# Hybrid RWKV/SSD/attention backbone on one core: the modulation sums beside the first RWKV layer's projections by transposed blocks, row sums and a band product

## What is computed

```python
silu_c = jax.nn.silu(c)
silu_cc = jax.nn.silu(c_ctx)
for i in range(DEPTH):
    ml = jnp.split((silu_c @ ada_w[i] + ada_b[i])[:, None, :], 6, axis=-1)
    mc = jnp.split(silu_cc @ ada_w[i] + ada_b[i], 6, axis=-1)
    hl = modulate(xl, norm1_g[i], ml[0], ml[1])
    hc = modulate(xc, norm1_g[i], mc[0], mc[1])
    ...
```

```python
dx = token_shift_centred(h) - h
xr, xw, xk, xv, xa, xg = (h + dx * mu[i] for i in range(6))
r = heads(xr @ wr); k = xk @ wk; v = heads(xv @ wv)
... xw @ w1[d] ... xa @ a1[d] ... xg @ g1
```

## Time and profile before

| what | value |
|---|---|
| median of 3 runs | 3931.67 us (3929.08 to 3935.01) |
| the profiled execution's own time | 3929.94 us |
| its span, first to last instruction | 3928.3 us |
| PE busy | 3809.7 us, 97% |
| DVE busy | 2364.5 us, 60% |
| ACT busy | 1303.0 us, 33% |
| POOL busy | 299.6 us, 8% |
| mean granted TensorE clock | 0.990 |

### The profile page before, as it was taken

How to read it: one execution, slowest core, us unless ns; L and a number is a source line. 1 busy time by engine, 2 the same in 40 slices (tenths; PEclk the granted TensorE clock), 3 DMA queues, 4 the chain that set the end, 5 groups by cost and what they waited for, 6 DMA issues and landing times.

```text
span 3928.3 us, 83381 instructions
## 1 busy us (share of the span) xinstructions
PE 3809.7 (97%) x32803; PEld 2313.1 (59%) x32803; DVE 2364.5 (60%) x4233; ACT 1303.0 (33%) x2511; POOL 299.6 (8%) x246
## 2 busy tenths in 40 slices
PE   6999999999999999999999999999999999999998
PEld 2559888644445454545444456554444458888787
DVE  7947777487743667663877235477842437776431
ACT  4036666221101455531111014321100237775311
POOL 2001101000000233220000000000000000000000
PEclk8999999999999999999999999999999999999999
DMA  5620000054432333222444320144432320000354
GB/s 198 211 60 4 4 4 15 26 160 146 154 94 74 105 99 97 78 78 91 160 154 127 101 67 28 36 136 159 140 112 79 94 68 4 4 4 15 102 152 132
DMA packets 480958, 350.64 MB, mean 89 GB/s; under 512 B 24849, under 2 KB 450137, under 8 KB 478457
## 3 DMA queue, kind: packets, MB, share of 16 engines
q1 hardware_dynamic: 454632, 235.94, 20.8%
q0 software_dynamic: 26000, 110.06, 7.8%
HBM read 344.76 MB, written 1.18 MB: 88 GB/s over the span
## 4 chain that ended last, share of the span: by engine, by line
PE 80%; DVE 11%; ACT 6%; issue 1%; SPq 1%; DMA 1%; DVEq 0%; POOL 0%; ACTq 0%; POOLq 0%
PE PS L249 38%; PE PS L950 17%; PE PS L1948 15%; PE PS L1059 2%; PE PS L584 2%; ACT WORK L2220 1%; PE PS L1107 1%; DVE WORK L1686 1%; DVE WORK L1689 1%; DVE WORK L425 1%; PE PS L1428 1%; PE PS L1119 1%; DVE WORK L1713 1%; ACT WORK L1571 1%; DVE WORK L654 1%
## 5 line engine op out<-in xcount | busy, mean ns | idle before, releaser
L249 PE MATMUL PS<-H,WR 128*128 128x512 f32 (+1 forms) x3440 | 1350.7, 552 | 2.8 <-DVE WORK L862 2.8
L249 PEld LDWEIGHTS PS<-H,WR 128*128 128x128 f32 x3440 | 648.6, 190 | 657.4 <-issue 630.6
L950 PE MATMUL PS<-BIG,WR 128*128 128x512 f32 (+1 forms) x1736 | 669.6, 543 | 4.7 <-DVE X L926 2.6
L1948 PE MATMUL PS<-WORK 64*64 64x64 f32 (+2 forms) x13088 | 571.3, 225 | 15.6 <-ACT WORK L2220 9.6
L1948 PEld LDWEIGHTS PS<-WORK 64*64 64x64 f32 (+1 forms) x13088 | 480.0, 136 | 95.8 <-ACT WORK L2220 30.7
L950 PEld LDWEIGHTS PS<-BIG,WR 128*128 128x128 f32 x1736 | 326.4, 190 | 319.5 <-issue 300.9
L425 DVE SCALAR_TENSOR_TENSOR WORK<-WORK,SC 128x512 f32<-128x512 f32 (+1 forms) x630 | 406.5, 645 | 22.4
L847 ACT ACTIVATE WORK<-PS,WORK 128x512 f32<-128x512 f32 (+1 forms) x176 | 111.8, 635 | 842.0 <-DVE WORK L877 583.4
L2220 ACT ACTIVATE WORK<-PS 128x256 f32<-128x256 f32 (+3 forms) x720 | 244.6, 340 | 233.8 <-PE PS L1948 215.8
L926 DVE SCALAR_TENSOR_TENSOR X<-PS,MOD,X 128x256 f32<-128x256 f32 x96 | 46.5, 484 | 423.6 <-PE PS L950 417.3
L860 DVE SCALAR_TENSOR_TENSOR WORK<-PS,WORK 128x510 f32<-128x510 f32 (+1 forms) x176 | 120.1, 682 | 186.3 <-ACT WORK L847 177.4
(11 more groups left out here) (281 smaller groups left out, 4624.0 us busy)
## 6 DMA issues: line engine op xcount, KB each, us to landing
WR<-in_ffn_w_in_dram SPq DMA_DIRECT2D x352, 256.0 KB, 2.9
WORK<-in_ada_w_dram POOLq DMA_DIRECT2D x33, 2048.0 KB, 8.9
WR<-in_ffn_w_out_dram SPq DMA_DIRECT2D x160, 256.0 KB, 2.7
WR<-in_ssd_w_in_dram SPq DMA_DIRECT2D x96, 256.0 KB, 2.8
WORK<-in_ada_w_dram POOLq DMA_DIRECT2D x16, 1024.0 KB, 5.9
BIG<-scratch_dram POOLq DMA_DIRECT2D x8, 2048.0 KB, 8.2
BIG<-in_ada_w_dram SPq DMA_DIRECT2D x4, 2048.0 KB, 18.6
WR<-in_rw_wk_dram SPq DMA_DIRECT2D x32, 256.0 KB, 2.8
```

Of the source, the lines that this page charges most:

```text
L249: mm = pe.matmul(outs, WR[:, slot, k, 0:m], rhs(k), start=first and k == 0, stop=last and k == nk - 1)
L950: mm = pe.matmul(PS[:, bank, lo:T], WR[:, opened[label], k, :], rhs(8 * r + k), start=r == 0 and k == 0, stop=last and k == nk - 1)
L1948: return pe.matmul(o, lhs, rhs, start=start, stop=stop)
```

## The change

The rides of layer 0 take the FFN's form: behind each ride DVE makes a transpose of the accumulator (two inputs x 512 columns, as one of 128x1024) and a row sum, and PE makes four band products in place of the eight with the ones. PE waits for the label of the row sum, `rsum`, in place of that of the ride. There are a buffer of its own for the transpose, two for the row sums in turn, and one for a band, which DVE makes ahead of the first ride. The FFN's functions only take their buffers and labels as arguments; they do what they did.

```diff
--- before.py
+++ after.py
@@ -505,22 +505,30 @@
         ROWSUM = WORK[:, 10240:10272]
         BAND = WORK[:, 10272:10272 + 96]
 
-        def band():
+
+        MIX_TURNED = WORK[:, 11264:12288]
+        MIX_ROWSUM = [WORK[:, 12288 + 32 * n:12320 + 32 * n] for n in range(2)]
+        MIX_BAND = WORK[:, 12352:12448]
+
+        def band(dst):
             eye = half_const("id64")
-            v(vec.memset(BAND, 0.0))
-            v(vec.tensor_tensor(BAND[:, 32:64], eye[:, 0:32], eye[:, 32:64], ALU.add))
-
-        def turned_sum(tag, i):
-            v(vec.transpose(TURNED, ACC[:, 0].rearrange("p s c -> p (s c)")), None, i)
-            v(vec.reduce_sum(ROWSUM, TURNED.rearrange("p (b j) -> p b j", j=32), axis=AX_X), f"{tag}.rows", i)
+            v(vec.memset(dst, 0.0))
+            v(vec.tensor_tensor(dst[:, 32:64], eye[:, 0:32], eye[:, 32:64], ALU.add))
+
+        def turned_sum(acc, turned, rowsum, label, i):
+            v(vec.transpose(turned, acc.rearrange("p s c -> p (s c)")), None, i)
+            v(vec.reduce_sum(rowsum, turned.rearrange("p (b j) -> p b j", j=32), axis=AX_X), label, i)
+
+        def four_groups(bank, rowsum, window):
+            by_block = rowsum.rearrange("p (s m j) -> p j m s", s=2, m=4)
+            for j in range(4):
+                out, low = PS[64 * (j // 2):64 * (j // 2) + 64, bank, 0:8], 32 - 32 * (j % 2)
+                mm = pe.matmul(out, window[:, low:low + 64], by_block[:, j], start=j % 2 == 0, stop=j % 2 == 1)
+            return mm
 
         def ride_pe4(tag, i):
             pe.wait_ge(vec_done, C.at(f"{tag}.rows", i))
-            by_block = ROWSUM.rearrange("p (s m j) -> p j m s", s=2, m=4)
-            for j in range(4):
-                out, low = PS[64 * (j // 2):64 * (j // 2) + 64, ABANK, 0:8], 32 - 32 * (j % 2)
-                mm = pe.matmul(out, BAND[:, low:low + 64], by_block[:, j], start=j % 2 == 0, stop=j % 2 == 1)
-            mm.then_inc(pe_done, C.mark(pe_done, f"{tag}.a"))
+            four_groups(ABANK, ROWSUM, BAND).then_inc(pe_done, C.mark(pe_done, f"{tag}.a"))
 
         def ride_pe(tag, i, n):
             pe.wait_ge(vec_done, C.at(f"{tag}.acc", i))
@@ -867,11 +875,11 @@
             v(vec.tensor_copy(CW[:, 0:66], columns(3 * l + 1, 0, 66)))
             v(vec.tensor_copy(CW[:, 66:132], columns(3 * l + 2, 0, 66)), f"f{l}.cw")
             taps3 = CW[:, 0:132].rearrange("p (t h f) -> p h f t", t=3, h=2)
-            band()
+            band(BAND)
             with C.loop(vec, f"f{l}", NF // 2) as i:
                 if l + 1 < DEPTH:
                     ride_sum(f"f{l}", i, 4)
-                    turned_sum(f"f{l}", i)
+                    turned_sum(ACC[:, 0], TURNED, ROWSUM, f"f{l}.rows", i)
                 vec.wait_ge(act_done, C.at(f"f{l}.c11", i, 1))
                 for h in range(2):
                     v(vec.tensor_copy(CWj[:, :, h, :], taps3[:, h, bass.ds(i * 2, 2), :]), f"f{l}.cwj" if h else None, i)
@@ -2151,10 +2159,10 @@
                 done(mm(PS[:, 6, lo:T], G2A[:, j * P:j * P + P], GS[:, lo:T]), f"t{j}.gate")
 
             def ride(j):
-                pe.wait_ge(vec_done, C.at(f"{t}.ride{j}"))
+                pe.wait_ge(vec_done, C.at(f"{t}.rsum{j}"))
                 if j:
                     pe.wait_ge(vec_done, C.at(f"{t}.rows{j - 1}"))
-                done(over_partitions(5, ACC[:, j % 2], 4), f"rode{j}")
+                done(four_groups(5, MIX_ROWSUM[j % 2], MIX_BAND), f"rode{j}")
 
             opened = {}
 
@@ -2417,11 +2425,14 @@
                             v(vec.tensor_scalar(acc[:, s_], w, by, None, ALU.mult), label)
                         else:
                             v(vec.scalar_tensor_tensor(acc[:, s_], w, by, acc[:, s_], ALU.mult, ALU.add), label)
+                turned_sum(acc, MIX_TURNED, MIX_ROWSUM[r % 2], f"{t}.rsum{r}", None)
 
             def ride_rows(r):
                 vec.wait_ge(pe_done, C.at(f"{t}.rode{r}"))
                 mod_rows(0, 16 + 4 * r, 4, PS[:, 5, 0:8], f"{t}.rows{r}", None)
 
+            if l == 0:
+                band(MIX_BAND)
             for r in range(4):
                 if l == 0:
                     ride(r)
```

## The result

The changed kernel takes 3942.81 us (median of 7 runs, 3940.91 to 3948.65); the kernel before, in 7 runs, 3932.44 (3929.08 to 3935.82). The ratio is 1.0033 with a 95% interval of 1.0024 to 1.0042, so it is slower by 9 to 17 us; 12.3 were forecast. The profiled execution took 3941.99 us.

A forecast was written before the change was run, and what follows sets the result against it. It took PE and DVE as two engines at one speed in the first layer's projections. Queue +10.5 and clock +1.8 made 12.3 on the median 3931.67, thus 3944 us; range 3939 to 3948.5.

The forecast's parts named there:

- PE's slot falls to 0.34 and PE does not get it: Layer 0's rides: PE's slot falls from 1.70 to 0.34 us, 10.9 saved in all, yet PE waits for DVE.
- DVE's turn is 2.53 us a ride with no spread, its band 0.40: Layer 0's rides on DVE: transpose plus row sum add 2.53 us each, 20.3 in all; the band once, 0.40.
- Two waits: PE idles for DVE's mix of input 6: 12.8 us in projection w, 5.4 to 7.5 in g.
- The clock, + 1.8 (1.2 to 3.3): PE's clock falls to half behind both waits; hidden after the first, paid after the second: +1.8 us, bounds 1.2 and 3.3.
- the dense row: PE's matmuls from 74.91 us: 50 took 23.42 instead of 21.63 us, 1.8 lost for 3.9 us at 0.56.
- the sparse one: PE behind a 6.8 us idle stretch ending at 3046.78: clock 0.50 for 7.1 us, 6.5 busy; upper bound 3.3.
- + 10.5 by the queue: First layer's projections: DVE's added work delays its mixes, so v starts at 225.9 instead of 215.4 us.
- PE would set the pace: First rival: in the first layer's projections DVE's additions are hidden, v 7.9 us earlier, 3924 us; chance 4%.
- The clock stays up: Rival: DVE's delay in the first layer comes as worked out, without PE's clock falling, 3942 us; chance 10%.
- Part is given back later: Rival: a later stage, waiting for something else than PE, returns part: +4 to +8, 3936 to 3940 us; chance 6%.

The follow-up runs named there:

- e8_act_only: Changed kernel with all eight sums in the old form and ACT making each ride's two multiply-only products; ratio 0.9988 to the kernel before.
- e3_fill: The filled kernel: changed kernel with 13 and 5 unread PE products ahead of input 6 of w and of g; ratio 1.0024 to the kernel before.
- e4_first: Changed kernel with the new form in rides 0 to 3 only, the old in 4 to 7; ratio 1.0020 to the kernel before.
- e1_pe_only: Changed kernel without DVE's transposes and row sums, PE's band products reading 32 accumulator columns directly; ratio 0.9982 to the kernel before.
- e2_dve_only: Changed kernel with DVE's transposes and row sums made but unused, PE's sums in the old form; ratio 1.0023 to the kernel before.
- e6_two: Changed kernel with the new form in rides 5 and 6 only; ratio 0.9980 to the kernel before.
- e7_act: Changed kernel with the new form in rides 4 to 7 only and ACT making each ride's two multiply-only products; ratio 0.9982 to the kernel before.
- e5_last: Changed kernel with the new form in rides 4 to 7 only; ratio 0.9997 to the kernel before.

## Why the prediction was right, step by step

- *PE's slot falls to 0.34 and PE does not get it.* Held: 0.34, and DVE's half alone with PE's old form was no slower. The saving per ride was put too high: two units and a ride take 14.28 us in the trace after (98.22 to 112.50) and 15.52 before (99.87 to 115.39), so 1.24 a ride and 9.9 in all, not 1.36 and 10.9. The slot alone doesn't show that the two units, from their start to the next ride's product, take 13.93 us in place of 13.82. The + 10.5 hardly rests on it, since DVE sets both moments.
- *DVE's turn is 2.53 us a ride with no spread, its band 0.40.* Held: 1.245 and 1.220 again, and zero to input 6 of g is 225.11 - 76.18 = 148.93 us; forecast 223.8 - 74.87 = 148.9.
- *Two waits.* Held in place, with the third of 0.54 us not foreseen; w 13.49 for 12.8, g 4.70 for 5.4 to 7.5. In the profile after, the clock had not fallen at zero (21.73 us for 50 matmuls, where before they took 23.42), so PE was earlier at w, and it was at half speed longer behind the first wait (5.9 us, not 3.9), so it was later at g. Neither moved v, since DVE set both moments.
- *The clock, + 1.8 (1.2 to 3.3).* The mechanism was right, the size was low: 5.9 us at 0.50 behind the second wait, and 2.8 us between the changed kernel and the filled one. I had taken the dense row, 3.9 us at 0.56; the sparse one, 7.1 us, was as near. Its count of idle stretches is short, too: the four it names did have the clock at 0.50 behind them, but the trace has two more of over 3 us at its start (3.42 and 6.79 us, the latter ending at 10.46) with a granted clock of 1.00 behind them. By durations that value is doubtful: six matmuls of L333 took 4.29 us at 10.46 and 2.74 us at 37.24.
- *+ 10.5 by the queue.* 10.7 with the clock kept up.
- *PE would set the pace* (the first rival, priced - 7.9): it needs DVE's additions to cost nothing; with them left out it gives - 5.0, since even DVE's old queue takes the first half's slots.
- *The clock stays up*, as a rival: v would be at + 10.5; it was at + 12.7. *Part is given back later*: from the scan on the profiled execution is shorter by 2.8 us than it was before (13.5 + 1.3 at zero against 12.0 in the span). So it is in part luck that the forecast of 12.3 lies so near the measured 10.4 (by the medians): the clock cost 1 us more than forecast, and outside the stretch something was given back that was forecast at nothing. Before, the clock was 0.83 from 680 to 700 us, and it was 1.00 in the same work after:

```profile
680.00:700.00 20.00, 18.70 (x438) 0.83 0.01 3
```

```profile
694.00:714.00 20.00, 18.59 (x510) 1.00 0.01 3
```

These rows, of before and of after, are from the recurrence of layer 0, where no edit was made. Of the other profiled kernels one has the fall at the same place (e8_act_only, 0.83 from 680 to 700), two have it some 12 us later, as their stretch is (e3_fill, e4_first), and five don't have it; each has falls elsewhere, the changed kernel too (0.83 from 3240 to 3260). Such a fall can move a single execution by some us (0.83 over 20 us of nearly dense work is an estimated 3.4 us), and that is why the sizes above are taken inside the stretch. It was not tested whether these falls follow from the change; and the timed medians of most kernels lie up to 5 us below what their stretch alone would give (+ 10.4 for + 13.5, - 3.4 for 0.0, - 8.4 for - 3.1), which stays open. The clock elsewhere may be a part: over the runs of the kernel before, a mean granted clock lower by 0.001 goes with 2.4 us more, and e8_act_only's mean is 0.0007 higher than that of the kernel before, an estimated 1.7 of its 3.4 us.

The rule of the Trainium skill (Perfetto Trace Analysis, Identifying the Most-Contended Engine), read as the prediction's rival reads it, by PE's matmul share over the whole kernel, gave the wrong sign. For PE the section itself doesn't take that share as the measure of headroom; it names MFU (the share of the peak matmul rate) and the share of weight loads, and the latter was 59% against DVE's 60%, by which PE doesn't stand out. The same page's section Optimization Strategy speaks of regimes in which another engine is the contended one, and that fits this trace: in a period here DVE was busy 14.56 of 15.30 us, though PE was busy in all of it, and the change put 2.53 us more on DVE and took 1.24 from PE.

## What to carry to other kernels

Before moving work from the engine that never waits to one that waits a little, add up, between one hand-over and the next, what the second engine has left: here 1.3 us before w's last input against 10.5 added, while over the whole kernel it was idle 40% of the time. Do as many moves as that room holds (two of eight gained 2.5 us in the stretch, eight lost 12.7), or make room on a third engine first. And price a new wait of PE with the half-speed stretch behind it, here 5.9 us, thus some 3 us more than the wait.

## What the runs showed of the hardware that was not expected

The wait's length alone did not tell whether the clock fell: PE's waits of 2.33 and 2.80 us in the filled kernel left it at 1.00, as one of 2.59 did before, but in the kernel with PE's half alone waits of 2.48 and 0.39 us, with two matmuls between, were followed by 0.50 from 139 to 142 us. Around zero PE has short waits too: seven of 0.20 to 1.03 us between 62.8 and 74.9 us in the kernel before, with 1.1 to 2.1 us of work between. There the granted clock was 1.00 from 66 us on and fell at 75, with PE working without a break from 74.91 on. It fell so in four of the ten profiled kernels (23.3 to 23.4 us from zero to ride 0's product: before, e1_pe_only, e2_dve_only, e8_act_only). In e4_first, e6_two and e7_act it fell between 71 and 73 us, some 3 us before zero, and was back by zero; in the changed kernel, e3_fill and e5_last it was low until 71 to 74 us and stayed up from there. In these six the same work took 21.6 to 21.7 us. So the 1.7 us are a matter of when the fall comes, not of whether. And filling two waits with 18 products that nobody reads gave back 2.8 us of the stretch.
